# A two-layer decoder trunk with mixture-of-experts layers: routing by tile, ring slots freed by row block, row-half mixer weights

## The reference

```
layer 0: x += hgrn2(rms_norm(x))          # gated linear recurrence, 8 heads of 128
         x += moe(rms_norm(x))
k, v = heads of rms_norm(x) @ w_kv        # shared with layer 1
layer 1: x += attention(rms_norm(x) @ w_q, k, v, bias) @ w_o   # causal, one block of 256 keys
         x += moe(rms_norm(x))
moe(h):  g = argmax(h @ w_group + b)      # 1 of 4 groups, weight softmax(g)
         e1, e2 = top 2 of the 8 experts of group g, by h @ w_expert + b
         out = sum over both: weight * ((silu(h @ Wi[:, :512]) * (h @ Wi[:, 512:])) @ Wo)
```

## Time and profile before

| | us |
|---|---|
| three runs | 1275.2, 1273.73, 1274.07 (median 1274.07) |
| profiled execution, its own time | 1273.23 |
| its span | 1271.4 |
| TensorE busy | 894.1 (70%) |
| VectorE, ScalarE, POOL busy | 280.1, 120.5, 19.2 |
| transfers | 446.62 MB, mean 351 GB/s |

### The profile page before, as it was taken

The page is one execution under the profiler, slowest core; times in us unless marked ns, Lnnn a source line. Parts: engine busy times, 40 slices in busy tenths (PEclk is TensorE's granted clock), DMA queues, the critical chain, the costliest instruction groups (busy, mean ns, idle before and its releaser), DMA issues.

```text
span 1271.4 us, 12063 instructions
## 1 busy us (share of the span) xinstructions
PE 894.1 (70%) x5118; PEld 421.8 (33%) x5118; DVE 280.1 (22%) x449; ACT 120.5 (9%) x313; POOL 19.2 (2%) x23
## 2 busy tenths in 40 slices
PE   7999997755657466556479999776475656664756
PEld 6865655221213121222124455522131212222211
DVE  4358434202011020202031251420210202020202
ACT  1000011100000000010001132110000000000000
POOL 1000010000000000000000100000000000000000
PEclk9999998978778687887789999897887868888768
DMA  9793243899999999999999525389999999999995
GB/s 346 190 362 135 75 190 133 359 421 427 427 429 427 429 429 429 428 427 428 419 399 393 196 108 198 133 359 428 428 427 428 427 428 428 429 429 427 428 417 230
DMA packets 54161, 446.62 MB, mean 351 GB/s; under 512 B 4449, under 2 KB 6793, under 8 KB 29537
## 3 DMA queue, kind: packets, MB, share of 16 engines
q1 hardware_dynamic: 53136, 443.30, 84.3%
q0 software_dynamic: 976, 2.63, 1.3%
HBM read 443.28 MB, written 2.62 MB: 351 GB/s over the span
## 4 chain that ended last, share of the span: by engine, by line
DMA 47%; PE 43%; SPq 4%; DVE 3%; issue 2%; ACT 1%; DVEq 0%
PE ps L1016 42%; DMA ring<-in_moe_w_in 30%; DMA ring<-in_moe_w_out 16%; SPq L364 2%; SPq L301 2%; PE ps L1019 1%; DVE work L739 1%; DVE work L729 0%; DMA xs<-in_x 0%; DVE xs L953 0%; DVE work L648 0%; DVE work L722 0%; DVE work L724 0%; ACT work L496 0%; ACT work L486 0%
## 5 line engine op out<-in xcount | busy, mean ns | idle before, releaser
L1016 PE MATMUL ps<-ring,work 128*32 128x512 f32 (+1 forms) x3456 | 626.3, 706 | 331.0 <-DMA ring<-in_moe_w_in 241.2
L1016 PEld LDWEIGHTS ps<-ring,work 128*32 128x32 f32 (+1 forms) x3456 | 199.6, 138 | 711.0 <-issue 700.1
L1016 PE MATMUL ps<-work 128*128 128x128 f32 (+4 forms) x1090 | 191.8, 349 | 7.2 <-DVE work L729 2.2
L897 DVE TENSOR_SCALAR work<-work 128x512 f32<-128x512 f32 x16 | 6.8, 427 | 720.8 <-ACT work L544 720.8
L1016 PEld LDWEIGHTS ps<-work 128*128 128x128 f32 (+2 forms) x1090 | 136.7, 193 | 76.0 <-issue 71.5
L496 ACT ACTIVATE work<-ps,first 128x128 f32<-128x128 f32 x128 | 36.5, 368 | 298.2 <-PE ps L1016 298.2
L1016 PE MATMUL ps<-work,ring 128*128 128x256 f32 x256 | 55.8, 380 | 1.3 <-issue 1.3
L899 DVE RECIPROCAL work<-work 128x512 f32<-128x512 f32 x16 | 53.6, 3353 | 0.5
L1016 PEld LDWEIGHTS ps<-work,ring 128*128 128x128 f32 x256 | 48.5, 190 | 8.7 <-issue 2.2
L549 ACT COPY work<-ps 128x512 f32<-128x512 f32 x32 | 18.7, 585 | 333.4 <-PE ps L1016 333.4
L1019 PE MATMUL ps<-first,work 128*128 128x128 f32 x184 | 26.4, 290 | 16.1 <-DVE work L682 8.1
(11 more groups left out here) (114 smaller groups left out, 237.7 us busy)
## 6 DMA issues: line engine op xcount, KB each, us to landing
ring<-in_moe_w_in SPq DMA_DIRECT2D x120, 2048.0 KB, 20.2
ring<-in_moe_w_out SPq DMA_DIRECT2D x52, 2048.0 KB, 20.4
ring<-in_moe_w_in SPq DMA_DIRECT2D x16, 1024.0 KB, 19.5
ring<-in_moe_w_out SPq DMA_DIRECT2D x32, 512.0 KB, 15.2
ring<-in_hg_w_in SPq DMA_DIRECT2D x7, 2048.0 KB, 20.3
work<-in_moe_w_out SPq DMA_DIRECT2D x4, 2048.0 KB, 9.8
ring<-in_w_kv SPq DMA_DIRECT2D x4, 2048.0 KB, 19.6
ring<-in_hg_w_out SPq DMA_DIRECT2D x2, 2048.0 KB, 21.1
```

The costliest lines, as they stand in the source:

```text
L1016: return pe.matmul(o, l, r, start=start, stop=stop)
```

## The change

- **Routing by tile** (`projected_and_routed`, `routed`, `placed`, `gate_weights`). Logits, choice and positions are formed for tile 0 while tile 1 is projected. The choice uses VectorE's `max` (eight largest) on the 32 logits, those of other groups pushed to -3e38, and a key for ties. The weights of both tiles are formed later, after the first pick. The expert's norm weights are multiplied into the router's weights early in the kernel. The mean square moves from VectorE to ScalarE, the added eps to POOL.
- **Gather by tile.** `first_half` gathers tile 0's part of the first quad before tile 1 is routed. Columns 0 to 511 are scaled by VectorE, the rest is gathered in two parts and scaled by ScalarE.
- **Slots by row block.** In the first quad `up` runs row block by row block; after the first of four, `first_k_done` lets the first quarter of the next four chunks be loaded (`load_freed`), the rest after `rows_done`.
- **Pass path moved.** `over` and its branch stand ahead of the last body; `combine` follows `down` in the same quad; the sum is added to `xs` in four pieces, and stores and transposes follow piece by piece.
- **Half score levels.** From level 1 on, only every second block of `m` columns is computed and copied. Gate and value projections are interleaved (`VG`), and `silu_gate` follows levels 1, 3, 5 and 6.
- **Mixer row halves.** Output, k/v and q weights are loaded as 512 rows of all columns (`row_half`) and used by `project_rows`.

```diff
+VG = [(1, 0), (0, 0), (1, 1), (0, 1), (1, 2), (1, 3), (0, 2), (0, 3)]
...
+                def load_freed(r0):
+                    for part, ks in ((0, slice(0, 1)), (1, slice(1, KD // 2))):
+                        if part:
+                            sp.wait_ge(*expert_read(layer, 0, 0))
+                        else:
+                            sp.wait_ge(first_k_done, layer + 1)
+                        for r in range(r0, r0 + GRP):
+                            c = ring_chunk(layer, r, 0)
+
+                            def copy(dst, src):
+                                sp.dma_start(dst[:, ks, :], src[:, ks, :])\
+                                  .then_inc(loaded[c % RING] if part else first_part_in, 16)
+
+                            expert_chunk(layer, r % QC // GRP, GRP * (r // QC) + r % GRP, copy, chunk(c))
+
                 def load_next(r, it):
+                    if freed(r, it):
+                        if r == RING + EXTRAS:
+                            load_freed(r)
+                        return
...
-                over_quads(sp, body)
-                over(layer)
+                over_quads(sp, body, lambda: over(layer))
...
+            for w in (w_kv[:, 0:D], att_w_q[0], w_kv[:, D:2 * D], att_w_o[0]):
+                for j in range(2):
+                    load(c, rows_view(chunk(c)), row_half(w, j))
+                    c += 1
...
+            def ffn_roots(i):
+                for a in range(TT):
+                    pool.wait_ge(ms_ready, i + a)
+                    pool.tensor_scalar(ms[:, a:a + 1], ms[:, a:a + 1], EPS, None, ALU.add).then_inc(eps_added, 1)
+                    eps_steps[0] += 1
+                    pool.wait_ge(eps_added, eps_steps[0])
+                    pool.tensor_tensor(rstd[:, a:a + 1], ms[:, a:a + 1], mhalf[:, a:a + 1], ALU.pow).then_inc(rstd_ready, 1)
...
+                    act.wait_ge(x_added, 4 * layer + 2 * a + 2)
+                    act.activation(hn[:, a, :], xs[:, a, :], ACT.Square, scale=D ** -0.5,
+                                   accum_out=ms[:, a:a + 1]).then_inc(ms_ready, 1)
+                    act.wait_ge(nt_done, 2 * ((2, 6)[layer] + a) + 2)
+                    act.copy(hrT[:, 4:8, a * P:(a + 1) * P],
+                             ps[:, 2 * a + 1, :].rearrange("p (k t) -> p k t", t=P)).then_inc(hT_act, 1)
+                act.wait_ge(gap_ready, layer + 1)
+                act.activation(ex, gap, ACT.Exp).then_inc(gap_exp, 1)
...
+            def projected_and_routed(layer, i):
+
+                def normed_rows(a):
+                    dve.wait_ge(rstd_ready, i + a)
+                    dve.tensor_scalar(hn_rows[:, a], xs[:, a, :].rearrange("p (q k) -> p q k", k=KD), rstd[:, a:a + 1],
+                                      None, ALU.mult).then_inc(xn_ready, 1)
+
+                def router_columns(a):
+                    dve.wait_ge(nt_done, 2 * ((2, 6)[layer] + a) + 1)
+                    dve.tensor_copy(hrT[:, 0:4, a * P:(a + 1) * P],
+                                    ps[:, 2 * a, :].rearrange("p (k t) -> p k t", t=P)).then_inc(hT_dve, 1)
+
+                add_projection(layer, 0, 0)
+                add_projection(layer, 0, 1)
+                normed_rows(0)
+                router_columns(0)
+                add_projection(layer, 1, 0)
+                routed(layer, 0)
+                add_projection(layer, 1, 1)
+                placed(layer, 0)
+                router_columns(1)
+                normed_rows(1)
+                routed(layer, 1)
+                placed(layer, 1)
+
+            def routed(layer, a):
+
+                dve.wait_ge(rt_done, 2 * layer + a + 1)
+                link(dve.scalar_tensor_tensor(lg[:, a, :], ps[:, a, 0:NG + E], rstd[:, a:a + 1], br[:, layer, :],
+                                              ALU.mult, ALU.add))
+                link(dve.tensor_reduce(gmx[:, a:a + 1], lg[:, a, 0:NG], AX.X, ALU.max))
+                link(dve.scalar_tensor_tensor(gpr[:, a, :], lg[:, a, 0:NG], gmx[:, a:a + 1], prio[:, 0:NG],
+                                              ALU.is_equal, ALU.mult))
+                link(dve.tensor_reduce(gss[:, a:a + 1], gpr[:, a, :], AX.X, ALU.max))
+                link(dve.tensor_scalar(gneg[:, a, :], gpr[:, a, :], gss[:, a:a + 1], -3e38, ALU.is_lt, ALU.mult))
+                link(dve.tensor_tensor(le[:, a, :].rearrange("p (g e) -> p g e", g=NG),
+                                       lg[:, a, NG:].rearrange("p (g e) -> p g e", g=NG),
+                                       gneg[:, a, :].unsqueeze(2).to_broadcast([P, NG, EG]), ALU.add))
+                link(dve.max(top[:, a, :], le[:, a, :]))
+                link(dve.scalar_tensor_tensor(key[:, a, :], le[:, a, :], top[:, a, 1:2], prio, ALU.is_ge, ALU.mult))
+                link(dve.scalar_tensor_tensor(key[:, a, :], le[:, a, :], top[:, a, 1:2], key[:, a, :],
+                                              ALU.is_gt, ALU.add))
+                link(dve.max(ktop[:, a, :], key[:, a, :]))
+                dve.tensor_scalar(asg[:, a, :], key[:, a, :], ktop[:, a, 1:2], None, ALU.is_ge).then_inc(asg_ready, 1)
+
+            def placed(layer, a):
+
+                dve.wait_ge(pos_done, 2 * layer + a + 1)
+                link(dve.scalar_tensor_tensor(pos[:, :, a, :], ps[:, 6 + a, 0:E].rearrange("p (q e) -> p q e", e=GRP),
+                                              1.0, asg[:, a, :].rearrange("p (q e) -> p q e", e=GRP),
+                                              ALU.add, ALU.mult))
+                dve.tensor_tensor(pick[:, a], pos[:, 0, a].unsqueeze(2).to_broadcast([P, GRP, BLK]),
+                                  slot.unsqueeze(1).to_broadcast([P, GRP, BLK]), ALU.is_equal)\
+                   .then_inc(pick_ready if a else first_pick, 1)
+
+            def gate_weights(layer):
+
+                def each(v, n):
+                    return v.unsqueeze(2).to_broadcast([P, TT, n])
+
+                dve.tensor_tensor(gap[:, :, 0:NG], lg[:, :, 0:NG], each(gmx, NG), ALU.subtract)
+                dve.tensor_tensor(gap[:, :, NG:], le, top[:, :, 0:1].to_broadcast([P, TT, E]), ALU.subtract)\
+                   .then_inc(gap_ready, 1)
+
+                dve.wait_ge(gat_done, 2 * layer * QUADS + 1)
+                dve.tensor_tensor(xgT[:, 0, 0:4, :], ps[:, 2:6, 0:P],
+                                  wrow[:, layer, 0:4].unsqueeze(2).to_broadcast([P, 4, P]), ALU.mult)\
+                   .then_inc(first_rows, 1)
+
+                dve.wait_ge(gap_exp, layer + 1)
+                link(dve.tensor_reduce(gsm, ex[:, :, 0:NG], AX.X, ALU.add))
+                link(dve.tensor_tensor(le, ex[:, :, NG:], asg, ALU.mult))
+                link(dve.tensor_reduce(esm, le, AX.X, ALU.add))
+                link(dve.tensor_tensor(esm, esm, gsm, ALU.mult))
+                link(dve.reciprocal(esm, esm))
+                for a in range(TT):
+                    i = dve.tensor_scalar(wgt[:, :, a, :], le[:, a, :].rearrange("p (q e) -> p q e", e=GRP),
+                                          esm[:, a:a + 1], None, ALU.mult)
...
+                    def odd(v):
+                        return v.rearrange("p b (n two m) -> p b n two m", two=2, m=m)[:, :, :, 1, :]
+
+                    dve.copy_predicated(odd(sdiag), odd(masks[:, l:l + 1, :]).to_broadcast([P, 2 * H, P // (2 * m), m]),
+                                        odd(scored)).then_inc(pred_done, 1)
...
-                if l < 4:
-                    silu_gate(l)
+                if l and VG[l - 1][0]:
+                    silu_gate(VG[l - 1][1])
...
+            def project_rows(c, j, lhs, bank, a, half):
+
+                arrived(c)
+                for k in range(KD // 2):
+                    i = mm(ps[:, bank, :], lhs[:, j * (KD // 2) + k, a * P:(a + 1) * P],
+                           rows_view(chunk(c))[:, k, half * 512:(half + 1) * 512],
+                           j == 0 and k == 0, j == 1 and k == KD // 2 - 1)
+                return i
...
+                def asked(v):
+                    return v if l == 0 else v.rearrange("p (n two m) -> p n two m", two=2, m=1 << (l - 1))[:, :, 1, :]
+
                 for h in range(H):
                     for a in range(TT):
                         b = 2 * h + a
-                        i = mm(ps[:, b // 4, (b % 4) * P:(b % 4 + 1) * P], k3[:, h, a * P:(a + 1) * P],
-                               q3[:, h, a * P:(a + 1) * P])
+                        i = mm(asked(ps[:, b // 4, (b % 4) * P:(b % 4 + 1) * P]), k3[:, h, a * P:(a + 1) * P],
+                               asked(q3[:, h, a * P:(a + 1) * P]))
...
+                    for j in range(2):
+                        pe.wait_ge(oT_ready, 6 + 2 * j if layer else 2 * a + j + 1)
+                        for half in range(2):
+                            i = project_rows(c + j, j, lhs, 4 + 2 * a + half, a, half)
+                            if j:
+                                i.then_inc(pr_done, 1)
+                            if a and j and half == 0:
```

(50 more changed lines are left out.)

## The result

The changed kernel takes 1246.23 us (median of 4 runs, 1243.24 to 1247.66), the kernel before 1274.41 (1273.73 to 1275.2). Ratio 0.9773, 95% interval 0.976 to 0.9785. Predicted were 1239 us, with a range of 1229 to 1252: the direction and the range held, and the point was 7 us too low. In the profiled execution, 1243.24 us with a span of 1241.3, 30.1 us are gone where the sum had said 34.9.

A forecast was written before the change was run, and what follows sets the result against it. Bound: fixed-byte expert streams at about 428 GB/s plus three compute stages. Terms 2.6 + 1.0 + 11.2 + 6.3 + 0 + 11.6 + 2.2 = 34.9 us off 1273.23 gave 1238.3, predicted as 1239, range 1229 to 1252.

The forecast's parts named there:

- Score levels: Eight score levels: moving the gate work removes TensorE's waits for VectorE, 2.6 us gained; halved score matmuls gain nothing.
- the 36-column row: Routing, kernel before: 16 instructions with only 36 columns take 0.117 us each, so halving score columns was costed at nothing.
- Output projection: Layer 0: starting on half the transposed rows gains 1.0 us; tile 0's router delays the last `pr_done` 1.9 us, both layers.
- The net for VectorE: Routing, both layers: VectorE's chain through `routed` of tile 1 ends 7.1 us after the last `pr_done` (t).
- first release at t + 13.5: Routing: first expert slots freed 13.5 us after the last `pr_done` (t), with 3.0 us for the first row block.
- The DMA runs dry at t + 33.5 ... I take 0.5 us lost per layer, ends 0 and 4: Expert stream: loads run out 33.5 us after the last `pr_done`, about when `up_done` frees four more slots; 0.5 us lost.
- 0.4 us of DMA idle: Restart, each layer: DMA idles 0.4 us between the early 2.1 MB and the other 6.3 MB of the freed slots.
- rival 1: Restart partly given back: the first quad's other waits leave the DMA idle, 5 us more per layer, 1249 us; 17%.
- Boundary: MoE 0 to layer 1's mixer: moved check and piecewise adds start projections 5.4 us earlier; 6.3 us with the clock term.
- The second term: Boundary of the layers: the first two microseconds of projections no longer at half rate, 1.0 us gained.
- Tail: End of the kernel: earlier last add and quarter stores with fewer issues behind, 2.2 us gained (1 to 3).
- Attention: Layer 1 attention: `att_v` waits for two copies, the output projection starts without a 0.68 us wait; together 0.

The follow-up runs named there:

- the second-pick kernel: Changed kernel with VectorE's weighing of the first quad and its pick for the second put ahead of the pass count in both layers: 1239.65 us, ratio 0.9732.
- the two-block kernel: Changed kernel with the early release after two row blocks instead of one, so four loads of 1 MB then four of 1 MB: 1239.14 us, ratio 0.9723.

## Why the prediction was right, and where it was off

**Score levels.** 2.6 us predicted, 2.9 in the trace (84.64 us against 87.56 for all levels). The gate order carries 2.1 of it, shown by the pitches. Of the other 0.8, 0.56 is the wait ahead of the fifth level, which went with the masked copy that is shorter from level 3 on: only with the gates early did TensorE wait for it. With the gates in their new place the halves carry nothing, as predicted from the 36-column row. The working had the copy at half its time on every level; on levels 1 and 2 it still takes 2.45 and 2.44 us, which the new order hides. The stride of level 1 costs nothing either (3.68 us for 32). By the Trainium skill's rule ("Advanced Engine Details and Errata", Memory Cachelines), non-contiguous outputs slow matmuls significantly; no such slowing is in these rows.

**Output projection.** The wait for the first copy is 0.29 us instead of 0.78; the router of tile 0 ahead of the last quarter behaves as said (from the end of the levels to the last `pr_done` it is 41.5 us, 40.7 before).

**Routing.** The net for VectorE was right to half a microsecond. The step that failed is "first release at t + 13.5": t + 15.25 was measured here, and t + 13.7 to t + 15.3 in the sixteen releases of this code. I had given the gather 8 instructions at up to 0.19 us; 16 stood ahead of the first row block in TensorE's queue (two of the four 128-column pieces of the second half too), at 0.23 each. With the clock held the release comes at t + 12.25, so the low clock costs 1.5 to 3.0 us in this stage.

**The restart.** The larger miss is the step "The DMA runs dry at t + 33.5 ... I take 0.5 us lost per layer, ends 0 and 4". Measured was a loss of 3.95 and 3.49 us per stream, near the far end of 4. One half, roughly, was `up_done` at t + 36.5 where I had 33.5 to 35: the pick behind the pass count, and a gather at half rate behind it (the second-pick kernel). The other half was not in my working except as "0.4 us of DMA idle": 512 KB parts in front of 1536 KB parts cost about 2 us, and parts of 1 MB nothing (the two-block kernel). So what happened is rival 1, the restart partly given back; its price was 2.8 us per layer beyond the forecast instead of 5. I had given it 17%, too little: its condition, a margin of nil, stood in my own working. The range held because it took this rival in, not because the sum was right about the streams.

**Boundary.** 5.4 us predicted and measured (14.76 to 9.36), and 4.3 of them come back with the jump over the long body, so the reason given was right in the main: the branch has left. That the figures agree to a tenth is in part luck: the stretch is 9.1 to 10.0 us where the last `down` group ran at a low clock, as here, and 7.7 us in the four executions in which it ran at the full one. The second term, 1.0 for the full clock in the projections, measured 0.85 (128 instructions 55.17 us against 56.02). What I had not separated is that the jump costs, and not the check.

**Tail.** 2.2 predicted for finer adds and stores, 4.95 measured, of three parts. The last `down` group ran at full clock here (1.92 us against 3.33; `combine` took 3.70 in both). Of the twelve executions with this code in the tail eight are like that, with 8.8 us; in the other four the group ran wholly or in part at the low clock, and the tail is 10.2 to 10.5 us. So about 1.6 us are the clock of this execution and not the change. With the long jump put back the tail is 12.7 at the low clock, so about 2.3 are the jump, which I had not counted here. About 1.0 is left for the adds and stores (13.7 against 12.7), half of what I gave them. The kernel before has one trace only, so these parts are good to some tenths at best. The 2.75 us by which the tail beat the forecast hid a part of the miss in the streams.

**Attention** was costed at nothing. From the first projection to the last `pr_done` it is 130.3 us before (671.62 to 801.95) and 130.8 after (655.42 to 786.24), with 1.9 us of router in it that was not there before, as said; 1.4 us are gained, of which 0.85 is the clock in the projections.

## What to carry to other kernels

Releasing a buffer earlier helps only up to the point where the next release comes before the transfers that it allowed are done: work out that second release with the same care as the first, and check the size of each part against the time to the next. Where a dense stage follows a serial chain of small steps, look at the granted clock in that chain, and try whether keeping TensorE busy pays. Leave no jump over a long body between the last product of one stage and the first of the next. When a change moves a restart by some microseconds and the total by fewer, measure the length of the stream from its restart to its last byte: it shows at once whether the rest was given back.

## What the runs showed of the hardware

- With 14 dummy products of 128 columns per layer in TensorE's waits, the granted clock stays at 1.0 through the routing, where it was 0.50 for nearly 10 us; this was worth 8.9 us of 1245. A wait of 2.2 us behind that was followed by the full clock in layer 0 (32 instructions in 3.84 us) and by the low one in layer 1 (5.47 us).
- Four loads of 512 KB followed by four of 1536 KB moved 324 GB/s for 5 us at a DMA share of 0.93; four of 1 MB and four of 1 MB moved 426 or more in the same place. Why that stretch is slow is open.
- A jump over a long untaken body left TensorE idle for 3.42 us and at a low clock behind it (4.3 us at the boundary in all); a value load with a jump over one instruction costs nothing visible.
- `MAX8` over 32 elements takes 0.20 us on VectorE, the sum of one column on GpSimd 0.22.
- A masked copy of half the columns takes 2.45 us with blocks of one and 2.44 with blocks of two, about what the whole does (2.43); from blocks of four on 1.25.
